# Two attentions stepped through head by head, or through pairs of heads on halves of TensorE

## The chip, the cores and the metric

The kernel runs on one core of a Trainium2 chip. The metric is the device time of one execution in microseconds (us). The kernel before takes 1473.68 us, the median of 3 runs (1472.41 to 1476.11).

## What is computed

The program is two transformer blocks over 512 tokens of width 1024, all in fp32. The change touches the first block. It projects a normalised input `h` to two attentions of eight heads of 64 columns each, multiplies what they give by gates, and adds it to the residual:

```python
def _stick_breaking(q, k, v):            # attention "a"
    z = einsum('bhtd,bhsd->bhts', qb, kb) * scale
    mask = s_idx < t_idx
    log_1m = where(mask, log_sigmoid(-z), 0.0)
    after = cumsum(log_1m, reverse=True) - log_1m
    w = where(mask, exp(log_sigmoid(z) + after), 0.0)
    out = einsum('bhts,bhsd->bhtd', w, vb)

def _forgetting_attention(q, k, v, cum_log_f):   # attention "b"
    z = einsum('bhtd,bhsd->bhts', qb, kb) * scale
    z = z + cum_log_f[t] - cum_log_f[s]           # the decay sums
    z = where(s_idx <= t_idx, z, NEG_BIG)
    out = einsum('bhts,bhsd->bhtd', softmax(z), vb)

y_a = (from_heads(a) * silu(z_a)) @ w_o_sb
y_b = (from_heads(b) * silu(z_b)) @ w_o_fox
gates = sigmoid(g_logit + b_gate)                 # 16 tiles of 128 columns
merged = gates[0] * y_a + gates[1] * y_b
x = x + gate * (merged @ w_out)
```

The second block (a pooling mixer, an RWKV mixer, a differential attention, a cross attention over 256 memory tokens and a convolutional feed-forward layer) is the same in both kernels.

## The kernel before, in words

Activations lie with their columns on the 128 partitions and the 512 tokens along the free dimension, so a projection makes tiles of 128 columns by 512 tokens, and the contraction runs over eight slices `k` of 128 rows. Weights come from memory in chunks of 1 MB (two tiles), over a ring of three slots. Each weight and each `h` is split into a high and a low part; ScalarE makes the high part (`split_weights`, L979), GpSimd the low part (L2033), and TensorE multiplies high by high, high by low and low by high (`mm3`), 24 products for a tile. The chunk after next can be split once the chunk before it in the same high slot is used up.

The attentions don't split: they work on plain fp32 operands, and each fp32 product stands in the trace as two MATMUL records with a weight load each. Line 528 is the helper `mm`, by which every product is issued, line 535 the helper `turn`, by which every transpose is.

Each engine runs its own program in order, and semaphores join them. A `Ring` hands out PSUM banks in turn: `take` lets TensorE wait until the bank's last tile has been moved out, `full` lets a reader wait until TensorE has filled it, and `wait_out` waits until the reader has moved it. In the attentions before, scores use banks 0 to 2, the side projections bank 3, transposes banks 4 and 5, and the outputs banks 6 and 7.

`attend` runs over 8 heads x 4 blocks of 128 queries, 32 steps. Block `b` sees `128 (b + 1)` keys. In step `i` TensorE (a) makes the scores of step `i` as one product with 64 rows of contraction and up to 512 columns, the head's 64 rows being the lower or the upper half of the partitions, and adds the mask by a bf16 product on the diagonal block; (b) transposes the weights of step `i - lag`, a 128 x 128 block at a time; (c) multiplies the transposed weights of step `i - lag - 2` by the values, `b + 1` products into 64 rows of the output bank, the lower or the upper half; and (d) calls `fill(i)`, a piece of a projection that has nothing to do with these heads. The lag is 4 in "a" and 2 in "b". In "b" TensorE also spreads one row of the decay sums `nF` over all partitions for each head (a product with `head_row`), which ScalarE moves to `nF_bc`.

The fills of "a" are the values of "b" (`vb`, eight tiles of 128 tokens by 256 columns), the silu input of "b" (`zb`, four tiles, in three pieces each) and two tiles of the gate projection `g`; those of "b" are nine further tiles of `g`, in three pieces each (`SIDE_G = 11`). The remaining five tiles of `g` follow after the attentions as an ordinary projection.

Between the products, attention "a" needs for each step: ScalarE's Abs, Exp and Ln of the scores (L1169 to L1171), VectorE's softplus (L1639), scan (L1643) and subtraction (L1644), and ScalarE's Exp (L1177); VectorE moves the transposed weights out (L1601). Attention "b" needs VectorE's subtraction with running minimum (L1656), ScalarE's Exp with a row sum (L1219), VectorE's reciprocal and scaling (L1673, L1675); ScalarE moves the transposed weights out (L1016). The order on each engine is written out by hand in the loops over `i`; `silu`, `rows_out`, `gate_out` (L1187), `gate_inverse`, `split_weights` and `gated_high` are put between the steps. The first of the 32 steps of "a" stands at 219.64 us of the span and the last product of "b" ends at 474.11 us.

## Time and profile before

| what | us |
|---|---|
| median of 3 runs | 1473.68 |
| the profiled execution | 1473.38 |
| its span (first to last instruction) | 1471.5 |
| TensorE busy in the span | 1407.8 (96%) |
| VectorE busy | 653.8 (44%) |
| ScalarE busy | 560.2 (38%) |
| GpSimd busy | 544.1 (37%) |
| first block's attentions, first score to last value product | 219.64 to 474.11 |

The span and the execution's own time differ by 1.9 us, which lies around the span. Busy shares are averages over all stages. A MATMUL record lasts longer than the time after which the next one starts, since products are pipelined, so the cost of a product is read from the distance between starts. The profile also gives the clock that TensorE was granted: 1.00 is 2.4 GHz, 0.50 is 1.2 GHz.

### The profile page before, as it was taken

The numbers are of one execution on the slowest core, as the hardware profiler recorded it, in microseconds if no ns is written. First come the engines' busy times: TensorE is split into PE (matmuls) and PEld (weight loads), VectorE is DVE, ScalarE is ACT, GpSimd is POOL, SyncE is SP. The second block draws the span as 40 slices with busy tenths as digits, with TensorE's granted clock in tenths as the row PEclk, the third lists the DMA queues.
The fourth block names the chain that finished last, engine by engine and source line by source line (L and its number), as shares of the span: only waits on it lengthen the run. The fifth ranks groups of instructions, "written<-read, shape, count | busy, mean of one in ns | idle before, by whom it ended". The sixth has DMA issues, their size and how long they took to land.

```text
span 1471.5 us, 18459 instructions
## 1 busy us (share of the span) xinstructions
PE 1407.8 (96%) x7314; PEld 1101.1 (75%) x7314; DVE 653.8 (44%) x1101; ACT 560.2 (38%) x923; POOL 544.1 (37%) x437
## 2 busy tenths in 40 slices
PE   6999999999999999999888987998999999999999
PEld 6878877665666888787787855876887888888887
DVE  3330106663223165773535666433555566564000
ACT  5622426573455433423214546334433232232111
POOL 6454441122112445453503200343045455545443
PEclk9999999999999999999998998999999999999999
DMA  9753220010010232422001001231022232222222
GB/s 370 307 196 126 102 88 30 30 58 29 30 57 30 87 114 86 176 86 86 30 2 57 30 1 58 86 143 57 8 107 87 86 100 100 86 88 78 98 98 97
DMA packets 20481, 131.88 MB, mean 90 GB/s; under 512 B 2224, under 2 KB 2352, under 8 KB 7344
## 3 DMA queue, kind: packets, MB, share of 16 engines
q1 hardware_dynamic: 18864, 120.12, 22.7%
q10 hardware_dynamic: 1536, 10.62, 1.9%
q8 instruction: 58, 0.95, 0.3%
q14 instruction: 23, 0.19, 0.0%
HBM read 124.44 MB, written 6.29 MB: 89 GB/s over the span
## 4 chain that ended last, share of the span: by engine, by line
PE 89%; DVE 5%; ACT 3%; issue 1%; POOL 1%; DMA 0%; DVEq 0%; SPq 0%; ACTq 0%
PE bank L528 87%; PE bank L535 2%; DVE arena L1656 1%; POOL weights_low L2033 1%; ACT weights_high L979 0%; DMA arena<-in_mem 0%; POOL arena L2060 0%; DVE acc L1521 0%; DVE xres L1531 0%; DVE arena L1913 0%; DVE arena L1915 0%; ACT memory_high L1026 0%; DVE arena L1950 0%; ACT arena L1016 0%; DVE arena L1890 0%
## 5 line engine op out<-in xcount | busy, mean ns | idle before, releaser
L2033 POOL TENSOR_TENSOR weights_low<-weights,weights_high 128x512 fp32r<-128x512 f32 (+1 forms) x388 | 497.8, 1314 | 869.1 <-ACT weights_high L979 869.1
L528 PE MATMUL bank<-h_high,weights_high 128*128 128x512 f32 x880 | 357.5, 406 | 1.6 <-ACT arena L1187 1.6
L528 PE MATMUL bank<-h_high,weights_low 128*128 128x512 f32 x880 | 348.0, 395 | 0.0
L528 PE MATMUL bank<-h_low,weights_high 128*128 128x512 f32 x880 | 347.9, 395 | 0.0
L979 ACT ACTIVATE weights_high<-weights 128x2048 fp32r<-128x2048 f32 (+2 forms) x101 | 177.5, 1757 | 370.4 <-PE bank L528 357.0
L528 PE MATMUL bank<-arena 128*128 128x128 f32 (+7 forms) x1688 | 236.7, 297 | 11.9 <-POOL arena L2060 4.1
L528 PEld LDWEIGHTS bank<-arena 128*128 128x128 f32 (+3 forms) x1688 | 176.9, 174 | 54.8 <-issue 38.1
L528 PEld LDWEIGHTS bank<-h_high,weights_high 128*128 128x128 f32 x880 | 165.1, 188 | 50.8 <-issue 11.3
L528 PEld LDWEIGHTS bank<-h_high,weights_low 128*128 128x128 f32 x880 | 165.2, 188 | 40.6
L528 PEld LDWEIGHTS bank<-h_low,weights_high 128*128 128x128 f32 x880 | 165.2, 188 | 40.1 <-issue 2.6
L1016 ACT ACTIVATE arena<-bank 128x512 f32<-128x512 f32 (+3 forms) x132 | 61.7, 474 | 110.6 <-PE bank L528 72.4
L1601 DVE COPY arena<-bank 128x512 f32<-128x512 f32 (+3 forms) x78 | 42.9, 552 | 108.8 <-PE bank L528 94.9
L535 PE MATMUL bank<-consts,arena 128*128 128x128 f32 x352 | 62.9, 287 | 24.2 <-DVE arena L1915 14.0
L1709 DVE TENSOR_TENSOR xres<-bank,xres 128x512 f32<-128x512 f32 x24 | 16.6, 691 | 153.9 <-PE bank L528 153.9
L535 PEld LDWEIGHTS bank<-consts,arena 128*128 128x128 f32 x352 | 41.6, 146 | 37.8 <-DVE arena L1915 21.6
L528 PE MATMUL bank<-gact_high,weights_high 128*128 128x512 f32 x176 | 69.6, 396 | 0.0
L528 PE MATMUL bank<-gact_low,weights_high 128*128 128x512 f32 x176 | 69.6, 396 | 0.0
L528 PE MATMUL bank<-gact_high,weights_low 128*128 128x512 f32 x176 | 69.6, 395 | 0.0
L1656 DVE CUSTOM_DVE_ANT_0 arena<-bank,arena 128x128 f32<-128x128 f32 (+3 forms) x64 | 30.0, 488 | 84.5 <-PE bank L528 66.7
L528 PE MATMUL bank<-weights_high,h_high 128*128 128x256 f32 x192 | 58.3, 304 | 1.5 <-ACT arena L1016 1.0
L528 PE MATMUL bank<-weights_low,h_high 128*128 128x256 f32 x192 | 55.2, 288 | 0.0
L528 PE MATMUL bank<-weights_high,h_low 128*128 128x256 f32 x192 | 55.1, 287 | 0.0
(292 smaller groups left out, 1991.2 us busy)
## 6 DMA issues: line engine op xcount, KB each, us to landing
weights<-in_stream SPq DMA_DIRECT2D x83, 1024.0 KB, 4.8
weights<-in_down SPq DMA_DIRECT2D x16, 704.0 KB, 4.1
arena<-in_ada SPq DMA_DIRECT2D x8, 1024.0 KB, 12.3
arena<-in_ada SPq DMA_DIRECT2D x8, 512.0 KB, 8.0
h<-in_stream SPq DMA_DIRECT2D x2, 1024.0 KB, 9.1
xres<-in_x SPq DMA_DIRECT2D x1, 2048.0 KB, 29.8
x_kept<-xres ACTq DMA_DIRECT2D x1, 2048.0 KB, 7.2
xres<-x_kept ACTq DMA_DIRECT2D x1, 2048.0 KB, 7.7
```

The source lines that it names most:

```text
L528: ins = nc.tensor.matmul(o, lhsT, rhs, start=start, stop=stop, skip_group_check=skip)
L535: ins = nc.tensor.transpose(o, i, ident[0:rows, 0:rows])
L979: nc.scalar.activation(hi_of(c)[:, cols], raw_of(c)[:, cols], ACT.Copy)\
L1016: nc.scalar.activation(dst, s_, ACT.Copy).then_inc(ring_.out(key), 1)
L1601: nc.vector.tensor_copy(dst, o if src is None else src(o)).then_inc(ring_.out(key), 1)
L1656: nc.vector.tensor_tensor_reduce(neg[:, slot, 0:width], o[:, 0:width], bias, -scale, 3.0e38, ALU.add, ALU.min, lowest).then_inc(M.out(key), 1)
L1709: ins = tt(xres[:, m, :], o, xres[:, m, :], ALU.add)
L2033: nc.gpsimd.tensor_tensor(lo_of(c)[:, cols], raw_of(c)[:, cols], hi_of(c)[:, cols].bitcast(F32), ALU.subtract).then_inc(sem("weights_split ...
```

## The change

Both attentions step through 4 pairs of heads x 4 blocks, 16 steps. A new `PairRing` hands out two neighbouring PSUM banks together: scores use banks 0 and 1 or 2 and 3 (two pairs in flight), transposes banks 4 and 5 (one pair in flight), outputs bank 6, side projections bank 7. The two heads of a pair have their scores made one right after the other, on the lower and the upper row half of TensorE, each into its own bank; the products with the values alternate between the two heads, which are the two column halves. The masks and the transposes are as many as before. `LAG` is 2 in both attentions, and the value products of step `i - 2` come after the fill of step `i`, in the same step as its transposes.

ScalarE's and VectorE's instructions take both heads' banks at once where they can (Abs, Exp, Ln, softplus, subtraction, moves); the scan, the subtraction with minimum, the Exp with row sum and the scaling stay one for each head. Attention "a" works in place in `pairs`, four slots of two heads, "b" in three.

The row of decay sums is no longer spread by TensorE and ScalarE. ScalarE's queue stores `nF` in memory (`nF_kept`) and reads two rows of it at a time to all partitions, at the start of "a" (pair 0), at its end (pair 1) and in steps 5 and 9 of "b" (pairs 2 and 3). `head_row` and its load go.

The side projections go in three parts of a tile, of which two stand together in every second step: a `vb` tile is now two token blocks in one bank, and `SIDE_G` is 8, so that eight tiles of `g` stand in "b", none in "a", and eight after the attentions. ScalarE moves the side tiles out, and the splits of their chunks are placed at steps 4, 5, 8, 9, 12, 13, 16 and 17.

```diff
...
+SIDE_G = 8
+PAIRS = HEADS // 2
+LAG = 2
+SLOTS_A, SLOTS_B = 4, 3
 XA_HEADS = 4
...
+SIDE_PARTS = (0, 6, 12, 16)
...
+                if b in second_of:
+                    pe.wait_ge(moved[second_of[b]], tiles[second_of[b]])
+                    del second_of[b]
...
+        class PairRing(Ring):
+            def take(self, pe, key):
+                b = self.banks[self.turn % len(self.banks)]
+                self.turn += 1
+                for i in range(2):
+                    if tiles[b + i]:
+                        pe.wait_ge(moved[b + i], tiles[b + i])
+                tiles[b] += 1
+                second_of[b + 1] = b
+                self.ids[key] = len(self.ids), b, tiles[b]
+                return bank[b], bank[b + 1]
+            def full(self, eng, key):
+                eng.wait_ge(self.filled, self.ids[key][0] + 1)
+                return two_banks[self.ids[key][1]]
...
+        nF_bc = [nF_rows, at(16896, 2, T)]
+        pairs, ptb = at(W1, SLOTS_A, 2, T), at(W1 + 4096, 2, 2, T)
         z_gate = at(16896, 2, T)
...
+        whole = [ctx.enter_context(nc.psum_tensor(f"banks{b}", [P, 2 * T], F32))[:, :] for b in range(0, 8, 2)]
+        two_banks = {2 * i: v.rearrange("p (a b) -> p a b", a=2) for i, v in enumerate(whole)}
+        bank = [whole[b // 2][:, T * (b % 2):T * (b % 2 + 1)] for b in range(8)]
...
+        F = Ring("side", [7])
+        M2, TR2 = PairRing("scores", [0, 2]), PairRing("turns", [4])
...
+            def side_part(key, m, part):
+                first, last = SIDE_PARTS[part], SIDE_PARTS[part + 1]
+                if part == 0:
                     if m % 2 == 0:
                         chunk[0] = next_chunk(KD, 256)
...
+                    side_bank[0] = F.take(pe, (key, m))
                 slot, w = chunk[0]
...
+                for i in range(first, last):
+                    if key == "vb":
+                        half, k = divmod(i, KD)
+                        if m % 2 == 0 and half == 0:
+                            split_ready(k, KD)
+                        mm3(side_bank[0][:, 256 * half:256 * (half + 1)], hrow(k, 2 * (m % 2) + half), [p_[:, k, :] for p_ in w],
+                            k == 0, k == KD - 1, F.filled if i == 2 * KD - 1 else None)
+                    elif i % 2 == 0:
+                        k = i // 2
+                        if m % 2 == 0:
+                            split_ready(k, KD)
+                        mm3(side_bank[0], [p_[:, k, P * (m % 2):P * (m % 2 + 1)] for p_ in w], h(k),
+                            k == 0, k == KD - 1, F.filled if k == KD - 1 else None)
+                if last == 2 * KD and m % 2 == 1:
...
+            def attend(tag, q, kk, v, mask, slots, weights_done, fill):
+                N = PAIRS * NB
+                for i in range(N + LAG):
                     if i < N:
...
+                        pair, b = divmod(i, NB)
+                        if b == 0:
+                            M.wait_out(pe, ("q" + tag, pair))
+                            M.wait_out(pe, ("k" + tag, pair))
+                        o = M2.take(pe, (tag, i))
                         end = P * (b + 1)
...
+                        for hh in range(2):
+                            lo, hi = head_rows(hh)
+                            mm(o[hh][:, 0:end], q[lo:hi, pair, P * b:end], kk[lo:hi, pair, 0:end], True, False)
+                        for hh in range(2):
+                            mm(o[hh][:, P * b:end], masks[:, 0, :], mask, False, True, M2.filled if hh else None)
+                    n = i - LAG
+                    if n >= 0:
                         pe.wait_ge(weights_done, n + 1)
...
+                        o = TR2.take(pe, ("T" + tag, n))
+                        for hh in range(2):
+                            for s in range(n % NB + 1):
+                                turn(o[hh][:, P * s:P * (s + 1)], pairs[:, n % slots, hh, P * s:P * (s + 1)],
+                                     TR2.filled if hh and s == n % NB else None)
+                    fill(i)
+                    if n >= 0:
+                        pair, b = divmod(n, NB)
+                        TR2.wait_out(pe, ("T" + tag, n))
+                        if b == 0:
+                            y = PV.take(pe, ("y" + tag, pair))
                         for s in range(b + 1):
...
+                            for hh in range(2):
+                                lo, hi = head_rows(hh)
+                                mm(y[lo:hi, P * b:P * (b + 1)], v[:, s, P * pair + lo:P * pair + hi],
+                                   ptb[:, n % 2, hh, P * s:P * (s + 1)], s == 0, s == b,
+                                   PV.filled if b == NB - 1 and s == b and hh else None)
+            def side(tile, i):
+                if i >= PAIRS * NB:
+                    return
+                part = (0, 1, 0, 1)[i % NB]
+                tile(i // 2, part)
+                if part == 1:
+                    tile(i // 2, 2)
+            PV.use([6])
+            for c in range(2):
+                for b in range(NB):
+                    M.wait_out(pe, ("va", c, b))
+            pe.wait_ge(sem("masks"), 3)
+            attend("a", qa, ka, va, masks[:, 1, :], SLOTS_A, sem("stick_w"),
+                   lambda i: side(lambda m, part: side_part("vb" if m < 4 else "zb", m % 4, part), i))
+            for m in range(4):
+                F.wait_out(pe, ("vb", m))
+            attend("b", qb, kb, vb, masks[:, 2, :], SLOTS_B, sem("fox_w"),
+                   lambda i: side(lambda m, part: side_part("g", m, part), i))
+            PV.use([6, 7])
...
+            def side_out(m):
+                if m < 4:
+                    c, half = divmod(m, 2)
+                    move(("vb", m), vb[:, 2 * half:2 * half + 2, 256 * c:256 * (c + 1)],
+                         lambda o: o.rearrange("p (b n) -> p b n", b=2), F)
+                else:
+                    move(("zb", m - 4), gated["b"][:, m - 4, :], None, F)
+            for i in range(N + 3):
+                if i % 2 == 0 and 2 <= i <= N:
+                    side_out(i // 2 - 1)
                 if i < N:
                     end = P * (i % NB + 1)
...
+                    e = pairs[:, i % SLOTS_A, :, 0:end]
+                    o = M2.full(act, ("a", i))
+                    if i >= SLOTS_A:
+                        TR2.full(act, ("Ta", i - SLOTS_A))
+                    link(nc.scalar.activation(e, o[:, :, 0:end], ACT.Abs))
                     link(nc.scalar.activation(e, e, ACT.Exp, scale=-1.0))
                     nc.scalar.activation(e, e, ACT.Ln, bias=1.0).then_inc(sem("stick_ln"), 1)
...
+                n = i - 1
                 if 0 <= n < N:
                     end = P * (n % NB + 1)
...
+                    M2.wait_out(act, ("a", n))
+                    w = pairs[:, n % SLOTS_A, :, 0:end]
                     nc.scalar.activation(w, w, ACT.Exp).then_inc(sem("stick_w"), 1)
...
+                if i == 1:
+                    act.wait_ge(sem("nF_ready"), 1)
+                    act.dma_start(nF_kept, nF[0:HEADS, :]).then_inc(sem("nF_stored"), 16)
+                if i == 4:
+                    act.wait_ge(sem("nF_stored"), 16)
+                    act.dma_start(nF_bc[0], nF_kept[0:2, :].partition_broadcast(P)).then_inc(sem("nF0_loaded"), 16)
+                if i % 4 == 0 and 4 <= i <= N:
+                    split_weights(0, 2)
+                if i % 4 == 1 and 4 <= i <= N + 1:
+                    split_weights(1, 2)
+                if i % 2 == 0 and 10 <= i <= N:
+                    silu("b", i // 2 - 5)
...
+            act.wait_ge(sem("silu"), 8)
+            act.dma_start(nF_bc[1], nF_kept[2:4, :].partition_broadcast(P)).then_inc(sem("nF1_loaded"), 16)
...
+                if i % 2 == 0 and 2 <= i <= N:
+                    gate_out(i // 2 - 1)
+                n = i - LAG
                 if 0 <= n < N:
                     end = P * (n % NB + 1)
...
+                    move(("Tb", n), ptb[:, n % 2, :, 0:end], lambda o: o[:, :, 0:end], TR2)
+                if i < N:
+                    end = P * (i % NB + 1)
+                    M2.wait_out(act, ("b", i))
+                    for hh in range(2):
+                        c = 2 * (i % SLOTS_B) + hh
+                        w = pairs[:, i % SLOTS_B, hh, 0:end]
+                        nc.scalar.activation(w, w, ACT.Exp, scale=-1.0, bias=small[:, 8 + c:9 + c],
+                                             accum_out=small[:, 14 + c:15 + c]).then_inc(sem("fox_exp"), 1)
+                if i in (5, 9):
+                    pair = i // 4 + 1
+                    M2.wait_out(act, ("b", NB * (pair - 1) - 1))
+                    act.dma_start(nF_bc[pair % 2], nF_kept[2 * pair:2 * pair + 2, :].partition_broadcast(P))\
+                        .then_inc(sem(f"nF{pair % 2}_loaded"), 16)
+                if i % 2 == 0 and 2 <= i <= N:
+                    gate_inverse(i // 2 - 1)
+                if i % 4 == 0 and 4 <= i <= N:
+                    split_weights(0, 2)
+                if i % 4 == 1 and 4 <= i <= N + 1:
+                    split_weights(1, 2)
                 if i % 4 == 3 and i < N:
...
+                    gated_high(i // 4)
...
+            for i in range(N + LAG + 2):
+                n = i - LAG - 1
+                if 0 <= n < N and n % NB == NB - 1:
+                    o = PV.full(dve, ("ya", n // NB))
+                    g = gated["a"][:, n // NB, :]
+                    tt(g, o, g, ALU.mult).then_inc(PV.out(("ya", n // NB)), 1)
+                n = i - LAG
                 if 0 <= n < N:
                     end = P * (n % NB + 1)
...
+                    move(("Ta", n), ptb[:, n % 2, :, 0:end], lambda o: o[:, :, 0:end], TR2)
                 if i < N:
                     end = P * (i % NB + 1)
...
+                    o = M2.full(dve, ("a", i))
+                    w = pairs[:, i % SLOTS_A, :, 0:end]
                     dve.wait_ge(sem("stick_ln"), i + 1)
...
+                    link(stt(w, o[:, :, 0:end], 0.0, w, ALU.max, ALU.add))
+                    for hh in range(2):
+                        v = w[:, hh, ::-1]
+                        ins = nc.vector.tensor_tensor_scan(v, ones(end), v, 0.0, ALU.mult, ALU.add)
+                    link(ins)
+                    tt(w, o[:, :, 0:end], w, ALU.subtract).then_inc(M2.out(("a", i)), 1)
+                if i % 2 == 0 and 10 <= i <= N:
+                    silu("b", i // 2 - 5)
...
+            for i in range(N + LAG + 2):
+                n = i - LAG - 1
+                if 0 <= n < N and n % NB == NB - 1:
+                    o = PV.full(dve, ("yb", n // NB))
+                    g = gated["b"][:, n // NB, :]
+                    tt(g, o, g, ALU.mult).then_inc(PV.out(("yb", n // NB)), 1)
                 if i < N:
...
+                    pair, b = divmod(i, NB)
                     end = P * (b + 1)
                     if b == 0:
...
+                        dve.wait_ge(sem(f"nF{pair % 2}_loaded"), 16 * (pair // 2 + 1))
+                    if i >= SLOTS_B:
+                        TR2.full(dve, ("Tb", i - SLOTS_B))
+                    else:
+                        TR2.full(dve, ("Ta", N - SLOTS_A + i))
+                    o = M2.full(dve, ("b", i))
+                    for hh in range(2):
+                        c = 8 + 2 * (i % SLOTS_B) + hh
+                        ins = nc.vector.tensor_tensor_reduce(pairs[:, i % SLOTS_B, hh, 0:end], o[:, hh, 0:end],
+                                                             nF_bc[pair % 2][:, hh, 0:end], -1.0, 3.0e38, ALU.add, ALU.min,
+                                                             small[:, c:c + 1])
+                    ins.then_inc(M2.out(("b", i)), 1)
                 n = i - 1
                 if 0 <= n < N:
                     end = P * (n % NB + 1)
...
+                    c = 2 * (n % SLOTS_B)
+                    dve.wait_ge(sem("fox_exp"), 2 * n + 2)
+                    link(nc.vector.reciprocal(small[:, 48 + c:50 + c], small[:, 14 + c:16 + c]))
+                    for hh in range(2):
+                        w = pairs[:, n % SLOTS_B, hh, 0:end]
+                        ins = ts(w, w, small[:, 48 + c + hh:49 + c + hh], None, ALU.mult)
+                    ins.then_inc(sem("fox_w"), 1)
...
```

## Rows read from the trace of the kernel before

**Rows 1.** Page, chain that ended last: share of the span by engine
```profile
PE 89%; DVE 5%; ACT 3%; issue 1%; POOL 1%; DMA 0%; DVEq 0%; SPq 0%; ACTq 0%
```

**Rows 2.** Windows: attention "a", attention "b" (busy us and instructions; then clock, DMA share, GB/s)
```profile
219.64:347.11 127.47, 123.42 (x673) 85.90 (x673) 80.67 (x138) 75.83 (x160) 23.29 (x17) 0.99 0.10 34
347.11:474.11 127.00, 125.20 (x569) 76.75 (x569) 34.12 (x131) 64.98 (x148) 25.22 (x20) 0.99 0.12 42
```

**Rows 3.** Timeline of TensorE inside "b" (start, us to last end, what)
```profile
390.52 1.12 PE L528 MATMUL bank<-arena,consts 8*128 8x512 f32 x2
391.57 0.48 PE L528 MATMUL bank<-arena 64*128 64x128 f32 x2
391.99 0.23 PE L528 MATMUL bank<-masks 128*128 128x128 bf16 x1
392.06 0.50 PE L535 MATMUL bank<-consts,arena 128*128 128x128 f32 x3
392.49 0.43 PE L528 MATMUL bank<-arena 128*64 128x128 f32 x2
392.85 0.50 PE L528 MATMUL bank<-h_high,weights_high 128*128 128x512 f32 x1
...
395.15 0.70 PE L528 MATMUL bank<-arena 64*128 64x256 f32 x2
...
402.76 1.12 PE L528 MATMUL bank<-arena 64*128 64x512 f32 x2
403.82 0.23 PE L528 MATMUL bank<-masks 128*128 128x128 bf16 x1
403.88 0.39 PE L535 MATMUL bank<-consts,arena 128*128 128x128 f32 x2
404.20 1.09 PE L528 MATMUL bank<-arena 128*64 128x128 f32 x8
405.22 1.12 PE L528 MATMUL bank<-arena,consts 8*128 8x512 f32 x2
```

**Rows 4.** Timeline of TensorE in the second block: products that alternate between halves
```profile
859.11 0.45 PE L528 MATMUL bank<-arena 64*64 64x64 f32 x8 [0.27 <-DVE arena L1890]
859.49 0.49 PE L528 MATMUL bank<-xres 64*128 64x128 f32 x4
859.91 0.45 PE L528 MATMUL bank<-arena 64*64 64x64 f32 x8
...
874.63 1.13 PE L528 MATMUL bank<-xres 64*128 64x512 f32 x4
```

**Rows 5.** Timeline of TensorE near the start: four products on four column quarters
```profile
51.65 1.06 PE L528 MATMUL bank<-arena,params 128*32 128x512 f32 x8
```

**Rows 6.** Groups by shape, 220 to 466 us: VectorE and ScalarE (busy, mean ns, idle before)
```profile
L1643 DVE TENSOR_TENSOR_SCAN arena<-consts,arena 128x512 f32<-128x512 f32 x8 | 11.9, 1488 | 0.3
L1643 DVE TENSOR_TENSOR_SCAN arena<-consts,arena 128x384 f32<-128x384 f32 x8 | 7.7, 958 | 0.3
L1643 DVE TENSOR_TENSOR_SCAN arena<-consts,arena 128x128 f32<-128x128 f32 x8 | 3.4, 425 | 0.3
L1644 DVE TENSOR_TENSOR arena<-bank,arena 128x512 f32<-128x512 f32 x8 | 5.5, 691 | 0.3
L1644 DVE TENSOR_TENSOR arena<-bank,arena 128x128 f32<-128x128 f32 x8 | 2.3, 291 | 0.3
L1170 ACT ACTIVATE arena<-arena 128x512 f32<-128x512 f32 x8 | 5.0, 631 | 0.3
L1170 ACT ACTIVATE arena<-arena 128x128 f32<-128x128 f32 x8 | 2.5, 310 | 0.3
```

**Rows 7.** Windows where TensorE waited and just after (columns as in rows 2)
```profile
226.00:228.00 2.00, 1.57 (x5) 0.68 (x6) 0.69 (x2) 1.94 (x6) 0.00 (x0) 1.00 0.00 0
...
230.00:232.00 2.00, 2.00 (x11) 2.00 (x11) 1.93 (x3) 0.00 (x0) 0.00 (x0) 0.52 0.00 0
```

**Rows 8.** DMA issues (KB each, median us from issue to landing)
```profile
arena<-in_ada SPq DMA_DIRECT2D x8, 1024.0 KB, 12.3
...
consts<-in_consts SPq DMA_DIRECT2D x1, 512.0 KB, 8.8
```

More of the change, by code:

```diff
@@ L119, in shape_constants @@
     put("restart", np.broadcast_to(tok % CHUNK != 0, (P, T)))
-    rows = np.zeros((P, HEADS, P))
-    for h in range(HEADS):
-        rows[h, h] = 1.0
-    put("head_row", rows)
     put("eps", np.full((P, 1), EPS))
```

184 lines of the change are left out of this document (21 added, 163 removed).

## The prediction

> **What bounds the kernel now.** I read the chain of waits first: TensorE holds 89% of the chain that ends last [rows 1], so a microsecond counts where TensorE is kept from its next product or has fewer of them. Next come the windows over the two attentions: they last 127.47 and 127.00 us, 254.5 together, and TensorE is busy for 123.4 and 125.2 of that [rows 2]. The reader is to see that the whole stretch is TensorE's own work, with only 5.9 us idle, while VectorE has 80.7 and 34.1 and ScalarE 75.8 and 65.0. Third comes the timeline inside "b", for the price of each kind of product, and last the rows of the second block, where halves of the array are already used side by side. Before it stands an unchanged projection, after it the gate projection, on which TensorE is dense too; so what the stretch gains, the kernel gains.
>
> **The prices, start to start [rows 3].** A head's scores: 0.42 us for 128 columns (391.57 to 391.99) and 1.06 for 512 (402.76 to 403.82), 0.63 and 0.85 between; 2.96 a head. A mask 0.07. Transposes: 0.43 for three, 0.32 for two, so 0.11 each and 0.10 once for the group. Value products: 0.36 for one block (two records), 1.02 for four; so 0.36, 0.58, 0.80, 1.02 and 2.76 a head. Spreading a row of decay sums: 1.05. Nine projection products of 512 columns take 2.30 (392.85 to 395.15), 0.233 each and 0.20 once for the piece.
>
> **Scores on row halves.** The differential attention of the second block already issues this pair. Four records of 64 x 128 take 0.42 us (859.49 to 859.91), as two do in the attention; four of 512 columns last 1.13 against 1.12 for two [rows 3, 4]. A pair costs what a head costs. The 16 heads of both attentions pay 16 x 2.96 = 47.4 now and 23.7 afterwards: 23.7 less. Bounds: 0 if the halves didn't overlap, 23.7 if fully.
>
> **Value products on column halves.** No row shows two fp32 products of 128 columns with a fresh weight load each on alternating halves. The nearest: four products on column quarters, 512 columns each, eight records in 1.06 us [rows 5], the time of one (1.06 above); and eight records of 64 x 64 that alternate in 0.38 (859.11 to 859.49) [rows 4], 0.048 each, where four products of 128 columns pay 0.127 a record in rows 3. I take full overlap, since both neighbours show it: 16 x 2.76 = 44.2 becomes 22.1. Bounds 0 and 22.1.
>
> The trace has 0.20 us of fixed cost in a projection piece that stands between products of other shapes [rows 3]. The Trainium skill (TensorEngine Tiling (Array Packing), Key Properties) says that a change of the tiling mode drains TensorE, while tiles of one mode work independently. By that rule the change gains twice, since 32 steps rather than 64 go through row halves, whole array and column halves; were the alternation itself a change of mode, nothing would be gained by pairs, which is the first rival below. Rows 4 are against that.
>
> **The rest of TensorE's work.** Eight products of decay sums go: 8.4. Transposes stay 160, but in 32 groups, not 64: 3.2. Masks stay 64. The side tiles stay the same work, in fewer pieces: `zb` and `g` had 15 x 3 pieces, now 12 x 2, and three `g` tiles stand in the plain projection behind: some 20 x 0.20 = 4.0. Sum of work removed: 23.7 + 22.1 + 8.4 + 3.2 + 4.0 = 61.4 us.
>
> **What the waits become.** The 9.5 us of waits and slow clock now in the stretch (5.9 idle [rows 2], and two times 3.4 us at half clock, from the 0.99 of both rows, about 1.8 each) were filled or caused by the old order; I take them out and work the new ones out. TensorE's new work is 254.5 - 61.4 - 9.5 = 183.6 us.
>
> A pair in "a" has 20.8 us of TensorE: scores 2.96, masks 0.52, transposes 2.5, values 2.76, two side tiles 12.0. By step (fill 2.3 in even, 3.7 in odd ones): 4.4, 6.4, 4.0, 6.0. VectorE's instructions on both heads cost, by the slopes of the instructions for one head [rows 6], 0.42, 0.69, 0.96 and 1.22 (three a step: softplus, subtraction, move), the scans 2 x 0.43 to 2 x 1.22 (0.425 and 0.958 at 128 and 384 columns; the mean of 1.49 at 512 says that some were longer): 16.5 a pair with 0.6 of links, silu and gating 18. ScalarE: Abs and twice the Exp of 1024 elements, 0.631 + 512 x 0.00084 = 1.06 each, so 3.25 in the last step.
>
> Only one place of "a" is short in each pair. In the last step (b = 3) scores take 1.2, ScalarE 3.25, VectorE 1.22 + 2.45 + 1.22 + 0.1 = 5.0: it ends 9.45 after the step's start; VectorE's next move (0.95) makes 10.4. TensorE reaches the value products that need this move at 6.0 + 3.6 = 9.6. So 0.8 us wait, three times; 2.4. Silu of ScalarE (three times 0.63) delays one of these by 1.0, and a long scan may add 1.
>
> The end of "a" is worse. After its last scores nothing fills: step 16 needs the move behind the last subtraction (10.4, with silu's delay 11.4). Then ScalarE does the last Exp (1.05), half a split (1.05) and silu 3 (2.0) to 14.5, and VectorE stands in the wait for silu with the last move queued behind it: 14.5 + 0.85 + 1.22 = 16.6, values 1.0, 17.6. TensorE's own work from there is 9.5: 8.1 us idle. Its first product of "b" stands behind it in its queue.
>
> In "b" VectorE has 9 us a pair and ScalarE 15 (move 2.8, Exp with sum 6.0, gates 4.0, split 2.1), against 20.8; no step is short, and at the end the two last moves wait for ScalarE, with a gate inverse and half a split ahead of the second: 2.4 us. The decay reads: pair 2's is issued in step 5, used in step 8, some 12 us later; loads of 512 KB and 1 MB land in 8.8 and 12.3 [rows 8], so nothing shows. If that cover were gone, each would cost its excess, once for each of two pairs.
>
> Sum of new waits: 2.4 + 1.0 + 1.0 + 8.1 + 2.4 = 15. **Clock.** After waits of 1.4 us in sum the granted clock fell from 1.00 to 0.52, which is the lower level, and stayed for 3.4 us [rows 7]; 512-column products then start 0.43 apart, so one fall costs 1.7. The end of "a" should bring two, the end of "b" one or none: 5 us. None of it is certain; 0 to 12.
>
> New stretch: 183.6 + 15 + 5 = 203.6, 50.9 less than 254.5. From the profiled execution's own 1473.4 (span 1471.5 and 1.9 around it) that gives 1422.5, and 0.3 more on the median's scale: **1423 us**.
>
> **Rivals.**
> First, the halves don't overlap, and the change doesn't do what it says. Then 45.8 come back, of which the longer steps hide 5 of the new waits: 1423 + 41 = 1464. For it: no row has this very shape. Against it: rows 4 and 5.
>
> Second, "a" becomes VectorE's and ScalarE's: the chain from scores to moved weights has two score slots and one slot of transposes, where the kernel before had three, two and a lag of 4. If each engine waits for the other some 4.4 us more a pair, a pair takes 26 and "a" 18 more: 1441. For it: VectorE's 18 of 20.8 leave 3. Against it: the one short place above is short by 0.8. The Trainium skill (TensorEngine Tiling (Array Packing), PSUM Bottleneck) warns that tiling speeds up TensorE but not the moves out of PSUM, which may then bound the stage. That speaks for this rival; VectorE's busy 80.7 of 127.5 us agrees so far that it is the nearest to the bound.
>
> Third, slower than before: in "a" the pair goes in lockstep, TensorE meeting each step's whole chain with nothing in flight. A pair would then be the sum: TensorE 20.8, Abs, Exp and Ln 8.9, VectorE 16.5, the last Exp 2.9: 49 instead of 21.6, 110 more: 1533. It decides from 12.7 us lost a pair (50.9 / 4). Against it: the second slot lets the next scores go out while VectorE works, and the fills (12.0 a pair) don't depend on the chain.
>
> **How the numbers follow.** My forecast 78%, the second rival 12%, the first 7%, the third 3%. A measurement of this kernel tells about 0.3% from no change, 4 us. Faster holds in all but the third: 0.96; same 0.01; slower 0.03. The range: below, the waits inside "a" go and the clock holds, 1423 - 15 = 1408; above, the second rival, 1443. It leaves out the first, the third and some edge.
>
> **What would show it.** Score pairs start to start as one head does (0.42 to 1.06), value products of four blocks near 1.0 for eight pairs of records: else the first rival. The stretch near 204 us. A wait of about 8 us at the change from "a" to "b", released by VectorE's move L1601 behind silu, and about 0.8 once a pair. No record with `head_row`'s 8 x 128 shape, no wait of VectorE on the decay reads. After 680 us or so the old trace shifted by 51 us, with the same waits. Wrong: a wait in each step of "a" (second), or a stretch over 254 us (third).

## The result, and the profile after

The changed kernel takes 1420.47 us (median of 4 runs, 1419.25 to 1421.11) against 1474.89 (1472.41 to 1476.48) for the kernel before on the same chip: ratio 0.9631, 95% interval [0.9614, 0.9649]. The forecast was 1423. The span of the profiled execution is 1418.0 us, 53.5 less than 1471.5.

The page's first lines of the changed kernel, busy time by engine (us, share of the span, instructions), and the chain that ended last (shares of the span, which answer to [rows 1]):

```profile
PE 1347.2 (95%) x7298; PEld 1078.4 (76%) x7298; DVE 647.5 (46%) x1037; ACT 546.3 (39%) x835; POOL 543.6 (38%) x437
PE 87%; DVE 6%; ACT 4%; issue 2%; POOL 1%; DMA 0%; DVEq 0%; SPq 0%; ACTq 0%; POOLq 0%
```

TensorE still bounds the kernel (1407.8 us busy before, 1347.2 now). VectorE has lost 6 us of busy time, ScalarE 14.

The windows over the attentions, which answer to [rows 2]: most of "a", the change from "a" to "b", and "b":

```profile
218.62:302.28 83.66, 78.98 (x582) 61.38 (x582) 65.88 (x83) 60.63 (x89) 17.26 (x13) 0.98 0.13 45
302.28:320.00 17.72, 11.51 (x61) 8.67 (x61) 8.56 (x12) 6.05 (x11) 5.11 (x4) 0.61 0.25 90
320.00:399.26 79.26, 77.22 (x511) 54.97 (x509) 31.95 (x111) 53.31 (x113) 17.07 (x14) 1.00 0.18 67
```

The attentions take 180.6 us instead of 254.5, but three tiles of `g` now stand behind them. The reader is to see that TensorE idles 4.7 of 83.7 us in the first window and 2.0 of 79.3 in the last, but 6.2 in the 17.7 us in the middle, where it is granted 0.61 of its clock. Which instructions it waits for there and elsewhere, all waits of TensorE in 218.6 to 399.3 (us in total, times, longest):

```profile
PE banks L550 <- DVE arena L1642: 10.5, 5, 4.2
PE banks L550 <- ACT arena L1042: 2.0, 2, 1.1
PE banks L550 <- ACT arena L1179: 1.0, 1, 1.0
PE banks L557 <- ACT arena L1215: 0.4, 1, 0.4
```

L1642 is VectorE's move of the transposed weights (L1601 before), L1042 ScalarE's move of the same in "b", L1215 the Exp of step 14 of "a". The wait on L1179 ends where the first scores start; inside the attentions the waits are 12.9 us. TensorE's timeline at the three short places inside "a" and at the change to "b" (L550 is `mm`, L557 is `turn`; one row runs together what touches the same names, so 16 records here are the value products of two or more blocks with the next pair's scores):

```profile
240.15 1.29 PE L550 MATMUL banks<-arena 128*64 128x128 f32 x14 [1.12 <-DVE arena L1642]
...
261.52 1.51 PE L550 MATMUL banks<-arena 128*64 128x128 f32 x16 [1.15 <-DVE arena L1642]
...
283.67 1.70 PE L550 MATMUL banks<-arena 128*64 128x128 f32 x16 [2.06 <-DVE arena L1642]
...
302.28 0.88 PE L557 MATMUL banks<-consts,arena 128*128 128x128 f32 x6 [0.35 <-ACT arena L1215]
307.38 1.55 PE L550 MATMUL banks<-arena 128*64 128x128 f32 x12 [4.22 <-DVE arena L1642]
```

VectorE at the same place:

```profile
305.24 1.23 DVE L1690 TENSOR_TENSOR arena<-banks,arena 128x1024 f32<-128x1024 f32 x1
306.38 0.95 DVE L1642 COPY arena<-banks 128x768 f32<-128x768 f32 x1
310.38 1.25 DVE L1647 TENSOR_TENSOR arena<-arena 128x512 f32<-128x512 f32 x1 [3.05 <-ACT arena L1136]
311.55 1.21 DVE L1642 COPY arena<-banks 128x1024 f32<-128x1024 f32 x1
```

The move for step 14 stands behind the last subtraction (L1690), and the last move behind silu (L1647), which waits 3.05 us for ScalarE. This is the wait that the prediction described.

TensorE in "b", which answers to [rows 3]:

```profile
383.85 0.92 PE L550 MATMUL banks<-arena 64*128 64x384 f32 x4
384.70 0.28 PE L550 MATMUL banks<-masks 128*128 128x128 bf16 x2
384.82 0.39 PE L557 MATMUL banks<-consts,arena 128*128 128x128 f32 x2
384.97 0.48 PE L550 MATMUL banks<-h_high,weights_high 128*128 128x512 f32 x1
...
392.84 0.66 PE L550 MATMUL banks<-arena 128*64 128x128 f32 x8
393.43 0.88 PE L557 MATMUL banks<-consts,arena 128*128 128x128 f32 x6
395.20 0.88 PE L550 MATMUL banks<-arena 128*64 128x128 f32 x12 [0.90 <-ACT arena L1042]
396.01 1.09 PE L557 MATMUL banks<-consts,arena 128*128 128x128 f32 x8
398.24 1.09 PE L550 MATMUL banks<-arena 128*64 128x128 f32 x16 [1.14 <-ACT arena L1042]
399.26 0.50 PE L550 MATMUL banks<-h_high,weights_high 128*128 128x512 f32 x1
```

A pair's scores of 384 columns take 0.85 us (383.85 to 384.70), what one head's did. Value products of two, three and four blocks for both heads take 0.59, 0.81 and 1.02 (392.84 to 393.43, and so on), what one head's did. Two transposes take 0.15 us to the start of the fill (384.82 to 384.97), where the kernel before paid 0.32 for two [rows 3].

The reads of the decay sums that answer to [rows 8] (copies, KB each, median us from issue to landing):

```profile
forget_rows<-nF_kept ACTq DMA_DIRECT2D x2, 512.0 KB, 3.6
arena<-nF_kept ACTq DMA_DIRECT2D x2, 512.0 KB, 3.3
```

No wait of VectorE on them is in the trace.

### The profile page after: what moved, and what is told of

Same layout as the page of the kernel before. It is cut to its first block, busy times and chain, and to the rows that moved or that the text cites. A ratio compares the mean times of both kernels' runs of the same rounds, so it can differ in the third digit from the quotient of the medians.

```text
span 1418.0 us, 18166 instructions
## 1 busy us (share of the span) xinstructions
PE 1347.2 (95%) x7298; PEld 1078.4 (76%) x7298; DVE 647.5 (46%) x1037; ACT 546.3 (39%) x835; POOL 543.6 (38%) x437
## 4 chain that ended last, share of the span: by engine, by line
PE 87%; DVE 6%; ACT 4%; issue 2%; POOL 1%; DMA 0%; DVEq 0%; SPq 0%; ACTq 0%; POOLq 0%
PE banks L550 85%; PE banks L557 2%; DVE arena L1697 1%; DVE arena L1688 1%; ACT arena L1208 0%; ACT weights_high L1005 0%; ACT arena L1207 0%; POOL arena L2112 0%; DMA arena<-in_mem 0%; POOL weights_low L2085 0%; DVE arena L1685 0%; DVE acc L1562 0%; DVE arena L1642 0%; DVE xres L1572 0%; ACT arena L1209 0%
## 5 line engine op out<-in xcount | busy, mean ns | idle before, releaser
L550 PE MATMUL banks<-h_high,weights_high 128*128 128x512 f32 x880 | 355.7, 404 | 1.7 <-ACT arena L1235 1.7
L550 PE MATMUL banks<-h_low,weights_high 128*128 128x512 f32 x880 | 348.3, 396 | 0.0
L550 PE MATMUL banks<-h_high,weights_low 128*128 128x512 f32 x880 | 348.1, 396 | 0.0
L550 PE MATMUL banks<-arena 128*128 128x128 f32 (+7 forms) x1688 | 188.1, 300 | 22.6 <-DVE arena L1642 10.5
L550 PEld LDWEIGHTS banks<-h_high,weights_high 128*128 128x128 f32 x880 | 165.7, 188 | 45.6 <-issue 7.0
L550 PEld LDWEIGHTS banks<-h_low,weights_high 128*128 128x128 f32 x880 | 165.7, 188 | 40.9 <-issue 2.6
L550 PEld LDWEIGHTS banks<-h_high,weights_low 128*128 128x128 f32 x880 | 165.5, 188 | 40.6
L550 PEld LDWEIGHTS banks<-arena 128*128 128x128 f32 (+3 forms) x1688 | 152.8, 176 | 48.6 <-issue 23.8
L1042 ACT ACTIVATE arena<-banks 128x512 f32<-128x512 f32 (+4 forms) x104 | 54.8, 532 | 119.6 <-PE banks L550 66.1
L1642 DVE COPY arena<-banks 128x512 f32<-128x512 f32 (+3 forms) x62 | 40.6, 655 | 97.9 <-PE banks L550 93.6
L557 PE MATMUL banks<-consts,arena 128*128 128x128 f32 x352 | 61.2, 301 | 21.9 <-DVE arena L1967 13.2
L557 PEld LDWEIGHTS banks<-consts,arena 128*128 128x128 f32 x352 | 44.0, 154 | 35.1 <-DVE arena L1967 20.8
L550 PE MATMUL banks<-gact_high,weights_high 128*128 128x512 f32 x176 | 69.6, 396 | 0.0
L550 PE MATMUL banks<-gact_low,weights_high 128*128 128x512 f32 x176 | 69.6, 396 | 0.0
L550 PE MATMUL banks<-gact_high,weights_low 128*128 128x512 f32 x176 | 69.6, 395 | 0.0
L550 PE MATMUL banks<-weights_high,h_high 128*128 128x256 f32 x192 | 57.4, 299 | 0.5 <-ACT arena L1046 0.5
L550 PE MATMUL banks<-weights_low,h_high 128*128 128x256 f32 x192 | 54.5, 284 | 0.0
L550 PE MATMUL banks<-weights_high,h_low 128*128 128x256 f32 x192 | 54.4, 283 | 0.0
## 6 DMA issues: line engine op xcount, KB each, us to landing
arena<-in_ada SPq DMA_DIRECT2D x8, 1024.0 KB, 12.2
```

What stands on the lines that cost most here:

```text
L550: ins = nc.tensor.matmul(o, lhsT, rhs, start=start, stop=stop, skip_group_check=skip)
L557: ins = nc.tensor.transpose(o, i, ident[0:rows, 0:rows])
L1042: nc.scalar.activation(dst, s_, ACT.Copy).then_inc(ring_.out(key), 1)
L1642: nc.vector.tensor_copy(dst, o if src is None else src(o)).then_inc(ring_.out(key), 1)
```

## The experiments

Each edit is shown against the changed kernel unless it says otherwise. "Stretch" is the time from the first mask to the last value product of both attentions in the profiled execution, "rest" what follows the first product on the gated outputs, and "half clock" the time at the lower level in the stretch (with the `g` tiles behind it) and in the rest. For the kernels before and after, the stretch is 253.9 and 180.0, the rest 969.3 and 971.6, and half clock 6.8 and 38.1, and 17.1 and 44.4. The runs lie on several chips, so that differences between kernels are read from the stretch. A ratio is to the kernel before, with its 95% interval.

**Scores of the two heads apart.** One bf16 mask product over the whole array stands between them:

```diff
                         for hh in range(2):
                             lo, hi = head_rows(hh)
                             mm(o[hh][:, 0:end], q[lo:hi, pair, P * b:end], kk[lo:hi, pair, 0:end], True, False)
-                        for hh in range(2):
                             mm(o[hh][:, P * b:end], masks[:, 0, :], mask, ...)
```

> The kernel after, but the first head's mask stands between the two heads' scores, so that the row halves can't work side by side: scores, mask, scores, mask. My theory: the overlap of the halves is worth 23.7 us, and two more changes of shape in each of 32 steps cost some 0.1 us each, of which attention a hides a little in its waits: about +25 us, 1446. Rival (the gain comes from fewer steps and pieces, not from the halves): no change beyond those 5 us, 1425.

1441.26 us, 0.9763 [0.9739, 0.9788]. The stretch is 202.2, 22.2 longer. TensorE with the second head's scores now alone (512 columns, two records):

```profile
363.22 1.12 PE L550 MATMUL banks<-arena 64*128 64x512 f32 x2
364.27 0.23 PE L550 MATMUL banks<-masks 128*128 128x128 bf16 x1
```

The second head pays its whole 1.05 us. Row halves overlap fully when nothing of another shape stands between them. The waits inside the attentions are 9.7 us here and 12.9 in the kernel after, and half clock is 3.4 us less (up to 1.7 at half speed), so TensorE's work grew by some 27 us, an estimate: the 23.7 of the scores, and 0.11 for each of the 32 steps, in which the two masks take 0.16 (363.06 to 363.22 in this trace) and 0.07 instead of 0.12 together.

**Value products head by head**, the same products with the loops exchanged:

```diff
-                        for s in range(b + 1):
-                            for hh in range(2):
+                        for hh in range(2):
+                            for s in range(b + 1):
```

> The kernel after, but a step's value products run through one head's blocks and then through the other's, so that the column halves don't alternate. My theory: what overlaps is what TensorE holds ready for the other half; in the second block a half's products began beside the last three or so of the other half. Steps of one and two blocks then keep most of their overlap and steps of three and four lose part: about +8 us, 1428. Strict order (only neighbours overlap): +17, 1437. If alternating is worth nothing: 1420.

1424.69 us, 0.964 [0.9614, 0.9666]; the stretch is 184.8, only 4.8 longer. The time does not tell this from the kernel after, the stretch does. By step (values with the next scores, up to the mask), this kernel in "b":

```profile
338.89 1.78 PE L550 MATMUL banks<-arena 128*64 128x128 f32 x16
340.60 0.29 PE L550 MATMUL banks<-masks 128*128 128x128 bf16 x2
...
345.20 2.43 PE L550 MATMUL banks<-arena 128*64 128x128 f32 x20
347.56 0.28 PE L550 MATMUL banks<-masks 128*128 128x128 bf16 x2
```

and the kernel after:

```profile
336.77 1.51 PE L550 MATMUL banks<-arena 128*64 128x128 f32 x16
338.21 0.28 PE L550 MATMUL banks<-masks 128*128 128x128 bf16 x2
342.80 1.94 PE L550 MATMUL banks<-arena 128*64 128x128 f32 x20
344.68 0.29 PE L550 MATMUL banks<-masks 128*128 128x128 bf16 x2
```

The steps of one and two blocks cost the same in both, within 0.01 (1.43 and 1.01 after, 1.43 and 1.02 here); three blocks with the next scores cost 1.71 instead of 1.44, four 2.36 instead of 1.88. So the halves overlap although the heads don't alternate, as if TensorE began the second head's products while the first's still run, and only the third and fourth block lose. The exchange of loops is therefore no test of what the halves are worth; a later experiment divides them for good.

**Both at once.**

> The kernel after with both: the masks between the scores and the value products head by head. My theory: the sum of the two, about +33 us, 1453. The first rival of the prediction named 1464 for halves without any overlap.

1448.53 us, 0.9814 [0.9782, 0.9846]; the stretch 206.3, 26.3 longer, where the two parts make 27.0 (22.2 and 4.8): they add up.

**The order of the changed kernel's step in the kernel before**, fill between transposes and value products, head by head as it was:

```diff
                         transposes(("T" + tag, n), weights(n), n % NB + 1)
+                    fill(i)
                     n = i - lag - 2
...
-                    fill(i)
```

> The kernel before with one part of the change alone: the piece of projection in each step stands between the transposes and the value products and no longer behind the value products. No product is added or removed. My theory: the transposes, the projection and the masks all use the whole array, and a change to another shape of tile costs about 0.16 us; each step with a piece has one change less, 53 steps: 8 us less than before, 1466. Rival (what the pieces lost comes from their number alone): no change, 1474.

1465.92 us, 0.9931 [0.9912, 0.995]. The stretch falls from 253.9 to 245.9 at the same half clock (6.8). TensorE in this kernel:

```profile
390.21 0.60 PE L535 MATMUL bank<-consts,arena 128*128 128x128 f32 x4
390.57 0.48 PE L528 MATMUL bank<-h_high,weights_high 128*128 128x512 f32 x1
```

Four transposes take 0.36 us where three took 0.43 [rows 3]. The edit computes the same products; the whole array, column halves and row halves now follow each other once a step, where the whole array came twice. The loops have 53 pieces of filling: 8.0 / 53 = 0.15 us for each. The waits of TensorE are the same as before but for 0.1 us. This reordering alone gives 8 us in the kernel before.

**The spreading products put back in "b"**, two for each pair, ahead of its first scores; their result is read by nobody:

```diff
                         end = P * (b + 1)
+                        if tag == "b" and b == 0:
+                            for hh in range(2):
+                                mm(o[hh], ident[0:HEADS, :], q[0:HEADS, pair, :], True, True)
```

> The kernel after with eight products of 8 rows by 512 columns put back on TensorE in attention b, two ahead of the first scores of each pair, as the spreading of the decay sums had them; nobody reads what they make. My theory: b is TensorE's own work throughout, so they cost their whole 8 x 1.05 us: +8.4, 1429. Rival (b has room, as waits on ScalarE hide part): below +4, under 1425.

1433.5 us, 0.9686 [0.965, 0.9722], the stretch 192.2, 12.2 longer. TensorE where one pair of them stands, then windows of 2 us before, over and behind it (columns as in [rows 2]):

```profile
336.16 1.98 PE L550 MATMUL banks<-arena,consts 8*128 8x512 f32 x4
338.07 0.60 PE L550 MATMUL banks<-arena 64*128 64x128 f32 x4
```

```profile
334.00:336.00 2.00, 2.00 (x16) 1.39 (x14) 0.02 (x1) 1.55 (x5) 0.00 (x0) 1.00 0.00 0
336.00:338.00 2.00, 2.00 (x10) 0.67 (x4) 0.00 (x0) 0.36 (x1) 0.00 (x0) 1.00 0.35 70
338.00:340.00 2.00, 2.00 (x14) 1.71 (x13) 0.80 (x6) 0.00 (x0) 0.00 (x0) 0.58 0.97 406
```

Eight products cost 8.4 by the rows of before (1.05 each); here two take 1.91 from start to start at full clock, so 7.6. TensorE's waits are those of the kernel after. The other 3.8 to 4.6 fit the clock: half clock is 27.3 us against 17.1, which at half speed is up to 5.1, and it came for 3.4 us each time 0.2 to 1.0 us behind the last three of the four pairs, though TensorE was busy without a break (behind the first it was low already, from the change to "b"). The windows show much DMA traffic there too; the kernel after has windows with a DMA share of 0.78 at the same places (336 to 338 and 356 to 358) and a clock of 1.00, and the last fall had a share of 0.79 in the 2 us before it, so that traffic of this size alone doesn't do it.

**Silu 3 moved behind the last move of "a"** on VectorE:

```diff
-                if i % 2 == 0 and 10 <= i <= N:
+                if i % 2 == 0 and 10 <= i < N or i == N + 1:
```

> The kernel after, but VectorE's last silu of attention a stands behind its last move of transposed weights, not ahead of it. My theory: the wait at the end of a is a chain in which that move stood queued behind a wait for ScalarE's silu; without it the move can go when the transposes are ready, some 1.2 us earlier, and no more, since the last transposes themselves come late and at the half clock: 1419, hard to tell from no change in the total; the trace should show the wait of 1.99 us before the last value products gone or under 0.8. Rival (the wait is set by ScalarE's last Exp and split): it stays.

1417.48 us, 0.9595 [0.9563, 0.9628]. All TensorE's waits on the move, in the stretch, and the last of them:

```profile
PE banks L550 <- DVE arena L1642: 9.9, 5, 4.2
...
312.00 2.71 PE L550 MATMUL banks<-arena 128*64 128x128 f32 x20 [1.32 <-DVE arena L1642]
```

Only 0.6 us of wait goes (10.5 to 9.9, at the last move, 1.99 to 1.32, where under 0.8 was expected), and 1.9 of the stretch, in which half clock is 3.4 us less. Silu was in the queue ahead of the last move, as predicted, but costs no more than that; the wait of 4.2 belongs to the move behind the last subtraction. The difference in time to the kernel after is within the spread of runs.

**ScalarE moves the weights of the step of three blocks of each pair in "a"** (`n % NB == 2`), so that VectorE's longest subtraction has no move behind it:

```diff
+                n = i - LAG
+                if 0 <= n < N and n % NB == 2:
+                    end = P * (n % NB + 1)
+                    move(("Ta", n), ptb[:, n % 2, :, 0:end], lambda o: o[:, :, 0:end], TR2)   # ScalarE
...
-                    move(("Ta", n), ptb[:, n % 2, :, 0:end], lambda o: o[:, :, 0:end], TR2)   # VectorE
+                    if n % NB != 2:
+                        move(("Ta", n), ptb[:, n % 2, :, 0:end], lambda o: o[:, :, 0:end], TR2)
```

> The kernel after, but in attention a ScalarE, not VectorE, moves out the transposed weights of each third step (three blocks), right after the Abs, Exp and Ln of the step. My theory: TensorE's wait once a pair (1.1, 1.1 and 2.1 us in the trace) is for this move, which stands behind the longest softplus, scan and subtraction on VectorE; ScalarE is idle there. The three waits go, and the 4.2 at the end gets about 1 shorter: 3 to 5 us less, 1416. Rival (the second half of the prediction's rivals: VectorE bounds a as a whole): the wait comes back in the next step, 1420.

1415.91 us, 0.9584 [0.9551, 0.9617]; the stretch 174.2, 5.8 shorter, with 6.9 us less at half clock (10.2). TensorE's two largest waits:

```profile
PE banks L550 <- DVE arena L1646: 3.9, 2, 3.2
PE banks L557 <- ACT arena L1219: 3.0, 3, 2.7
```

The wait once a pair is gone but for 0.7 us, and all waits inside "a" are 1.2 us instead of 4.3, so the short place in each pair was the move behind VectorE's longest step. At the change to "b" the sum stays: 0.18, 0.90, 2.67 (the last Exp of "a") and 3.24 (the last move), 7.0 us instead of 6.6. There the queue before a move only decides which step of one long chain TensorE is seen to wait for.

**One run of 32 steps** instead of two of 16: the first two steps of "b" are issued before the last two of "a" are used up, and ScalarE's and VectorE's loops are joined likewise:

```diff
-            attend("a", qa, ka, va, masks[:, 1, :], SLOTS_A, sem("stick_w"), ...)
-            attend("b", qb, kb, vb, masks[:, 2, :], SLOTS_B, sem("fox_w"), ...)
+            for i in range(2 * N + LAG):      # step i of "a", then i - N of "b"
+                ...
```

> The kernel after with the two attentions joined to one run of 32 steps: the first two scores and fills of b stand ahead of the last two transposes of a, on ScalarE and VectorE the first two steps of b stand between the last ones of a, and VectorE's last silu of a stands behind its last move. No instruction is added or removed. My theory: the 6.6 us that TensorE waits at the change from a to b, and the 13.7 us at half clock behind them, come from the empty lag; filled, the waits go and most of the slow clock, 4 of 6.8 us: 10 us less, 1410. Rival (the waits move on, since the chain of the last step of a is as long as before): 3 us less or no change, 1417 to 1420.

1408.86 us, 0.953 [0.95, 0.9561]; the stretch 170.7, 9.4 shorter, half clock in it 3.4 instead of 17.1:

```profile
PE banks L550 <- DVE arena L1659: 6.4, 4, 2.1
```

No wait over 2.1 us is left; the waits inside the attentions fall from 12.9 to 8.4 us. The change from "a" to "b" cost 9.4 us, in waits and in the clock behind them. This kernel has silu 3 behind the last move too, which alone took 1.9 us off the stretch above, and that part is not told apart here.

**The last two edits together.**

> The joined kernel with ScalarE's moves too: the attentions as one run of 32 steps, and in attention a ScalarE moves out the transposed weights of each third step. My theory: the two gains are of different waits (the change from a to b, and the wait once a pair behind the longest step of VectorE), so they add but for the last pair, where both shorten the same wait: 4 us under the joined kernel, 1404. Rival (both take the same waits away): 1408.

1403.57 us, 0.9519 [0.9503, 0.9535]: faster than both kernels, and than the kernel after on the same chip (1418.87) by 15.3 us. Its window over the attentions:

```profile
218.63:384.07 165.44, 161.69 (x1153) 120.36 (x1153) 102.13 (x201) 122.26 (x216) 39.69 (x31) 1.00 0.18 65
```

TensorE is busy for 161.7 of 165.4 us at full clock: here the stretch has nearly reached its own work.

**The value products of the two heads divided** by a product of one column over the whole array:

```diff
+                        for hh in range(2):
+                            if hh:
+                                mm(o[0][:, 0:1], ident, ident[:, 0:1], True, True)
+                            for s in range(b + 1):
```

> The kernel after, but a step's value products run head by head, and between the two heads stands one product of the whole array with one column (its result is read by nobody), so that the column halves can't work side by side. My theory: with the first head's blocks still in the array when the second's begin, the run by blocks kept most of the overlap and cost 5 us only; here all of it goes: +22, and 32 times two changes of shape and the small product, some 0.3 us together, +10: 1445 to 1453. Rival (column halves overlap little in any order, and the 22 us of the prediction come from elsewhere): +10 at most, 1430.

1443.03 us, 0.9784 [0.9762, 0.9805]; the stretch 201.8, 21.8 longer. TensorE in a step of four blocks:

```profile
351.21 1.09 PE L550 MATMUL banks<-arena 128*64 128x128 f32 x8
352.23 0.38 PE L550 MATMUL banks<-consts 128*128 128x1 f32 x2
352.54 1.93 PE L550 MATMUL banks<-arena 128*64 128x128 f32 x12
354.41 0.28 PE L550 MATMUL banks<-masks 128*128 128x128 bf16 x2
```

The first head takes 1.02 us, and so does the second (1.87 with the next scores, whose 0.85 are in the row too); the dividing product takes 0.31. From the first value product to the mask it is 3.20 us where the kernel after has 1.88: 1.32 more, 1.02 + 0.30. Column halves do overlap, and what undoes it is a product of another shape between them. By that step the sum over all steps would be near 2.76 x 8 + 32 x 0.3 = 31.7; the stretch shows 21.8, since it also lost 5.5 us of waits and had 13.7 us less at half clock (up to 6.8 at half speed).

**The kernel after once more**, on the chip of the last two.

> The kernel after, unchanged, beside the other two on the same chip, as the measure for them: 1420.

1418.87 us, 0.9635 [0.9594, 0.9677]. The profile has the same stretch, 180.0, and the same half clock in it.

## Why the prediction was right

The forecast was right in time and in mechanism; one term of its sum was mis-sized.

**Scores on row halves, 23.7.** Shown: dividing them costs 22.2 us of stretch (some 27 of TensorE's work, less the waits and slow clock that went), and a pair starts its masks 0.85 us behind, as one head did.

**Value products on column halves, 22.1.** Shown: 0.59, 0.81 and 1.02 for a pair against 0.58, 0.80 and 1.02 predicted, and dividing them costs 1.02 us in a step of four blocks. The first rival (1464) is out.

**Decay sums, 8.4.** Shown within the clock's share: putting the products back costs 12.2 us of stretch, of which 7.6 to 8.4 are the products. The reads land in 3.3 to 3.6 us, where the prediction counted on a cover of 12; bounding them by 8.8 and 12.3 was too cautious, without effect.

**Transposes and pieces, 3.2 + 4.0: the term that was mis-sized.** The prediction put a fixed 0.20 us on a filling piece "that stands between products of other shapes" and counted only that there are fewer pieces. It left out that the fill now stands directly behind the transposes, which have its shape. The chain of waits has the transposes of one pair of "b" and of the next at:

```profile
324.95 0.23 PE banks L557 x2
...
344.96 0.22 PE banks L557 x2
```

A pair in "b" so takes 20.0 us, not 20.8. Over both attentions TensorE's work is 161.7 us (the joined kernel with ScalarE's moves has the same products and no half clock there) where the prediction has 183.6 - 16.8 = 166.8: 5.1 less. The same reordering in the kernel before saved 8.0 against the 4.0 for pieces, so most of this is shown; the other 1.1 is open.

**New waits, 15.** Measured 12.9. Once a pair in "a" it was 1.12, 1.15 and 2.06 (predicted 0.8 each, 1.0 for silu and 1.0 for a long scan, 4.4 in all, measured 4.3); the end of "b" 2.0 (2.4); the change to "b" 0.35 + 4.22 + 1.99 = 6.6 (8.1). The last was put down mainly to the move queued behind silu. Moving silu away gave back 0.7 of it: the place and size were right, that reason for it mostly wrong. It is the chain from the last scores through VectorE's last scan, subtraction and moves with nothing left to fill, whatever stands in the queues (7.0 with one move on ScalarE); letting "b" begin under it removed it.

**Clock, 5.** The trace has 17.1 us at half clock, 3.4 from 284.8 and 13.7 from 305.3. In 304 to 318 TensorE was busy for 8.63 us at 0.55 of its clock, so about 4.3 are the clock's, and 1.7 the other's: 6.0. TensorE is busy for 167.7 us in the three windows, which is 6.0 more than the 161.7 at full clock.

**Together.** The stretch with the `g` tiles was 199.6 (180.6 and 19.0 for three tiles more behind it) against 203.6: 4.0 shorter, which is 5.1 from TensorE's work, 2.1 from waits, less 1.0 of clock and 2.2 for the `g` tiles, whose two waits on `gate_out` (1.7 in sum) were not foreseen. With 1.0 us of earlier start, 55.8 were gained up to the first product on the gated outputs. The span fell by 53.5: 2.3 came back later, in code that is the same in both. There half clock is 44.4 us instead of 38.1, which at half speed is up to 3.1, and TensorE is busy for 928.0 us instead of 924.5 with as many records. In all kernels here this rest lies between 969.3 and 973.9, with 38 to 51 us at half clock; that a shift in time is what moves these stretches is argued, not shown. The forecast is so closer in sum (2.6 us of span) than in its terms: 8.2 us that it did not have (work 5.1, waits 2.1, start 1.0) stand against 5.5 the other way (clock 1.0, `g` tiles 2.2, the later code 2.3). That these nearly cancel is luck.

**The second and third rival** (1441, 1533). "a" is nearest to VectorE's bound where the forecast had it, once a pair, but from one short place to the next it takes 21.4, 22.2 and 23.7 us (240.15, 261.52, 283.67, 307.38), the last with the wait at the change to "b", and not 26 or 49. The Trainium skill (TensorEngine Tiling (Array Packing), PSUM Bottleneck) warned of the moves out of PSUM; the trace agrees in kind, as all 10.5 us of the largest wait are on such moves, and outside the change to "b" such waits are 4.3 us in "a" and 2.0 at the end of "b", of 180.6.

## What to carry to other kernels

Where heads have 64 columns, issue the two heads of a pair on row and on column halves with nothing of another shape between them: a pair then costs what a head cost. Order each step so that everything of one shape stands together, fills included. When the engine that bounds a stage gets faster, look at the seams between loops first: here joining two loops and moving one copy to another engine gave 15 us more. TensorE's idle time inside the attentions fell from 12.9 to 3.8 us, and the 17.1 us at half clock went too.

## What the runs showed of the hardware

- A filling piece moved behind products of its own shape saves TensorE 0.15 us (8.0 us for 53 pieces, one change of the array's shape fewer for each). This is no price for every change: two changes more in a step, for a mask between the two heads' scores, cost 0.11 together.
- fp32 products of 128 columns on the two column halves overlap even when one half's come first, for up to two blocks (four records) a head; with three and four they lose 0.27 and 0.48 us of 0.80 and 1.02. One product of a single column over the whole array between them takes away all of it.
- A read of 2 rows from memory to all partitions (512 KB) lands in 3.3 to 3.6 us, where one load of 512 KB at the start of the kernel before took 8.8.
- The granted clock fell to its lower level (1.2 GHz) for 3.4 us within 1.0 us behind two products with 8 rows, with TensorE busy for 100% of the 4 us before it, in three places of four (the fourth was low already); the windows of 2 us there show 0.53 to 0.58. In the kernel before, one such product stood alone in each of eight places (1.05 us), and the stretch had two falls in all. Why they come is open. With 6.6 us of waits between 302 and 313 it was low for 13.7 us from 305.3 on; behind one wait of 2.06 us it was low for 3.4.
